# Forty-nine low parts of weight tiles move from GpSimd to VectorE in a float32 transformer kernel

## The chip, the cores and the metric

One Trainium2 chip, one of its cores. The metric is the device time of one execution of the whole program in microseconds (us), as a median of runs. Five engines take part: TensorE (PE in the profile, with PEld for its weight loads), VectorE (DVE), ScalarE (ACT), GpSimd (POOL) and SyncE (SP), which issues the weight loads.

## What is computed

The reference runs two transformer blocks in float32 on one sequence of 256 tokens of width 1024.

- First block, layer 0: a gated causal convolution of 31 taps over 768 channels beside an attention to 256 memory tokens, an output projection, and an MLP with squared ReLU of width 4096.
- First block, layer 1: shared keys and values (with a small compression MLP), sparse attention (compressed, selected and windowed branches, gated) beside a second memory attention, an output projection, and a second MLP of the same kind.
- Second block: "stick-breaking" attention beside a latent attention with rotary positions, an output projection, a gated MLP with a short causal convolution (`up` and `down`), and a gated embedding projection (`ple`, `ple_gate`).

```
x = first_block(x, mem, ...)      # two layers: x + mix @ w_out;  x + square(relu(norm(x) @ w_in)) @ w_out
return second_block(x, p_2, ...)  # x + norm(mix @ w_o);  x + norm(f @ w_down);  x + norm(g * e)
```

## The kernel before, in words

All activations lie in the on-chip memory (SBUF) in transposed form: 8 tiles of 128 channels by 256 tokens. Only the weights stream. They come in blocks (mostly 1024 rows by 256 columns, 1 MB) through a ring of four buffers, `ring`. SyncE issues the load of block b when block b-4 has been used up (`block_done`, L556).

**Weight tiles and their two parts.** A block holds two weight tiles w and w+1, each 128x1024. Products keep nearly float32 precision by splitting each operand into a high part, rounded to the matmul's format `fp32r`, and a low part, the difference. ScalarE makes the high part of tile w (`split_high`, L582, activation at L592). Then VectorE or GpSimd makes the low part, `ring - split_hi`, a tensor_tensor with both inputs in SBUF (`split_low`, L594, instruction at L600). TensorE multiplies high by high, high by low and low by high (`product`, L712, or `half_products`, L725; the matmuls stand at L707). High and low parts lie in four slots each (`SPLIT` = 4), so tile w+4 can be split when TensorE is done with tile w.

**Who makes a low part.** `low_part_engines()` (L396) writes down an engine for each of the 280 weight tiles. GpSimd has three shares: all tiles beside the convolution at the start (22 tiles, w = 4 to 25), the odd tiles beside the stick attention (6 tiles, in `s_in`, `s_lat`, `s_val`), and, of all other stages but `up`, each tile with w % 4 == 1 from w = 29 on (49 tiles). VectorE has the remaining 203.

**Where in an engine's program it happens.** GpSimd's program is little else: it walks through its tiles in order (`low_parts`, L1930), and each waits for its high part alone. VectorE's and ScalarE's programs are written out by hand in stage order, and a call `pump(stage, t)` (L1996 for VectorE, L1415 for ScalarE) stands behind the work on output tile t: it splits the tile four places later. On VectorE a pump of a tile that GpSimd has is empty. So the order of VectorE's work around a moved tile is fixed by these calls:

- `residual(stage, ...)` (L2033), used for `out0`, `out1` and the last eight tiles of each MLP: per tile t it adds the two halves of the result to x, then makes the low part of x's tile t-1 for the next stage (`low_of_x`, L2004), folds its squares into a sum (`fold`, L2015), then pumps t-1. `low_of_x` and `fold` read two SBUF operands.
- `mlp(l, ...)` (L2281): per tile of `mlp_in` it adds the two halves, applies ReLU and the norm's factor, makes the low part of hidden tile t-2 (`low_hidden`), and pumps t. In layer 1 a piece of `rope_angles` (L2252) follows in tiles 8 to 15.
- The start of layer 1 (L2318 to L2455): after `kv` it pumps tiles of `b_in`, forms the compression windows by 16 small additions (L2338), inverts the norm `ks` (L2341), makes two low parts of the values, pumps `b_in` 0 and 1 (L2348), then scales the keys (L2352), which ScalarE copies next. After query tile 7 it pumps `b_in` 4 and 5 (L2442), then forms `vbd` (L2446), which ScalarE copies ahead of the softmax work.
- The end of `down` (L2824 to L2843): residual additions with a `fold` each, then `pump("down", 21)`, the inversion of `postffn`, two more pumps and the norm.

TensorE's waits for a low part are on a count of the engine that makes it (`low_ready`, L573): `low_vector` or `low_gpsimd`. SyncE waits on the same counts for both halves of a block before it loads over it.

Of the kernel before, what the change touches and what calls it, by code (L numbers as in the profile page):

```python
# [26 lines left out]
SPLIT = 4  # L27
# [368 lines left out]
def low_part_engines():  # L396

    out = []
    for w, (_, _, (stage, t)) in enumerate(WEIGHT_TILES):
        beside_conv = w >= SPLIT and (stage in ("a_in", "mem_kv0", "mem_kv1") or (stage == "out0" and t < SPLIT))  # L400
        beside_sticks = w % 2 == 1 and (stage in ("s_lat", "s_val") or (stage == "s_in" and t >= SPLIT))
        out.append("gpsimd" if beside_conv or beside_sticks or (w >= SPLIT and w % 4 == 1 and stage != "up") else "vector")
    return out


LOW_ENGINE = low_part_engines()
LOW_COUNT = [LOW_ENGINE[:w + 1].count(LOW_ENGINE[w]) for w in range(NTILES)]
OUT = {name: n for n, name in enumerate(output_groups())}
# [2599 lines left out]
```

How the kernel before makes its waits and increments, by code:

```python
        def block_done(eng, b):  # L556
            name, r, _, c, _ = WEIGHT_BLOCKS[b]
            if name in DIRECT_LAST:
                wait_tile(eng, *DIRECT_LAST[name])
            elif name in DIRECT:
                if name == "gates":
                    eng.wait_ge(sem("gates.low_weights"), 1)
                elif r:
                    wait_tile(eng, name, 0)
                else:
                    eng.wait_ge(sem("compress_used"), 1 if name == "cmp_k" else 2)
            else:
                for half in range(2):
                    low_ready(eng, WEIGHTS_OF[tile_of(name, r, c)[0], tile_of(name, r, c)[1] + half])
# [1 line left out]
        def low_ready(eng, w):  # L573
            eng.wait_ge(sem(f"low_{LOW_ENGINE[w]}"), LOW_COUNT[w])
# [6 lines left out]
        def split_high(act, w):  # L582
            if w >= NTILES:
                return
            b = WEIGHT_TILES[w][0]
            act.wait_ge(sem(f"weights_in{b % RING}"), 16 * (b // RING + 1))
            if w >= SPLIT:
                wait_tile(act, *psum_of(*WEIGHT_TILES[w - SPLIT][2]))
            src, n = raw_weights(w)
            nc.scalar.activation(split_hi[:, w % SPLIT, 0:n], src, ACT.Copy).then_inc(sem("high_parts"), 1)
# [1 line left out]
        def split_low(eng, engine, w):  # L594
            if w >= NTILES or LOW_ENGINE[w] != engine:
                return
            eng.wait_ge(sem("high_parts"), w + 1)
            src, n = raw_weights(w)
            (nc.vector if engine == "vector" else nc.gpsimd).tensor_tensor(
```

## Time and profile before

| | |
|---|---|
| median of 3 runs | 1140.75 us (1138.5 to 1141.86) |
| the profiled execution's own time | 1141.37 us |
| its span, first to last instruction | 1139.6 us |
| TensorE busy | 1034.2 us, 91% of the span |
| VectorE busy | 814.0 us, 71% |
| ScalarE busy | 613.1 us, 54% |
| GpSimd busy | 192.8 us, 17% |
| low parts on VectorE (L600) | 203, mean 1231 ns |
| low parts on GpSimd (L600) | 77, mean 2464 ns |
| chain that ended last, by engine | PE 69%, DVE 22%, ACT 5%, issue 3% |

How to read it: "busy" is the time in which an engine executes. The granted clock is the share of its full 2.4 GHz that TensorE was given in a stretch. The chain of waits follows the program back from its last instruction. "Gap" or "idle before" is time in which an engine did nothing ahead of an instruction, with the instruction that ended the wait behind the arrow. Back-to-back instructions overlap a little: the pitch from start to start is shorter than the duration shown.

### The profile page before, as it was taken

Reading aid. Unit: us, or ns where it says so; the run is one execution under the profiler, and the core shown is the slowest. Engines: PE = TensorE matmul, PEld = TensorE weight load, DVE = VectorE, ACT = ScalarE, POOL = GpSimd, SP = SyncE. Lnnn points to the kernel's source line nnn. Section 1 sums busy time; section 2 is a strip of 40 time slices with the busy share of each in tenths; the row PEclk is TensorE's granted clock in tenths of the full one; section 3 lists DMA queues with packets and bytes.
Section 4 is the critical chain, followed back from the end, with each engine's and each line's share of the span. In section 5 each row is a group of like instructions: output and inputs, shape, how many; then the busy total and the mean of one; then the engine's idle time right before and its main releaser. Section 6 shows DMA issues by size and latency. Waiting matters only on the chain.

```text
span 1139.6 us, 17502 instructions
## 1 busy us (share of the span) xinstructions
PE 1034.2 (91%) x6654; PEld 931.8 (82%) x6654; DVE 814.0 (71%) x1571; ACT 613.1 (54%) x1147; POOL 192.8 (17%) x89
## 2 busy tenths in 40 slices
PE   5997689999999797878999999999988899999976
PEld 5996478888889796767887888898778799999865
DVE  4799778967768734685797766857645678777775
ACT  5552266654646545454655654665345566646555
POOL 1782002221212100000121222133000000010210
PEclk9996689999999897599999999999978999999978
DMA  8442024545445333101446555432301345554501
GB/s 350 155 176 76 1 74 181 196 180 204 167 181 185 112 116 112 37 1 37 157 179 219 181 189 185 184 119 77 137 13 74 130 177 180 184 192 169 194 33 37
DMA packets 22834, 158.28 MB, mean 139 GB/s; under 512 B 2528, under 2 KB 2784, under 8 KB 4448
## 3 DMA queue, kind: packets, MB, share of 16 engines
q1 hardware_dynamic: 21888, 153.51, 36.9%
q10 hardware_dynamic: 864, 3.66, 0.8%
q8 instruction: 53, 0.87, 0.3%
q14 instruction: 29, 0.24, 0.1%
HBM read 156.12 MB, written 1.05 MB: 138 GB/s over the span
## 4 chain that ended last, share of the span: by engine, by line
PE 69%; DVE 22%; ACT 5%; issue 3%; DMA 1%; DVEq 0%; ACTq 0%
PE bank L707 66%; DVE obank L1980 5%; DVE split_lo L600 3%; PE obank L707 2%; DVE square_sum L1972 1%; DVE temps L1972 1%; PE bank L840 1%; ACT split_hi L592 1%; DVE probs L1976 1%; DVE x L1972 1%; ACT L1388 1%; DVE tmp L1980 1%; DVE mlp_parts L1980 1%; DVE hidden_parts L1972 1%; DVE tmp L1972 1%
## 5 line engine op out<-in xcount | busy, mean ns | idle before, releaser
L707 PE MATMUL bank<-act_parts,split_hi 128*128 128x256 f32 (+1 forms) x1632 | 341.2, 305 | 32.5 <-DVE split_lo L600 13.1
L592 ACT ACTIVATE split_hi<-ring 128x1024 fp32r<-128x1024 f32 (+1 forms) x280 | 289.7, 1048 | 121.2 <-PE bank L707 120.7
L600 POOL TENSOR_TENSOR split_lo<-ring,split_hi 128x1024 fp32r<-128x1024 f32 (+1 forms) x77 | 189.3, 2464 | 910.7 <-ACT split_hi L592 910.7
L707 PEld LDWEIGHTS bank<-act_parts,split_hi 128*128 128x128 f32 x1632 | 270.3, 200 | 44.6 <-issue 28.7
L600 DVE TENSOR_TENSOR split_lo<-ring,split_hi 128x1024 fp32r<-128x1024 f32 (+1 forms) x203 | 247.8, 1231 | 38.0 <-ACT split_hi L592 37.1
L707 PE MATMUL bank<-hidden_parts,split_hi 128*128 128x512 f32 (+1 forms) x816 | 265.2, 377 | 2.9 <-DVE split_lo L600 2.2
L707 PE MATMUL bank<-act_parts,split_lo 128*128 128x256 f32 x880 | 256.1, 291 | 0.0
L707 PE MATMUL bank<-hidden_parts,split_lo 128*128 128x256 f32 x752 | 211.2, 281 | 0.0
L707 PE MATMUL bank<-mlp_parts,split_hi 128*128 128x512 f32 x512 | 181.0, 398 | 2.4 <-DVE mlp_parts L1980 2.4
L707 PEld LDWEIGHTS bank<-hidden_parts,split_hi 128*128 128x128 f32 x816 | 148.9, 188 | 34.0 <-DVE split_lo L600 2.8
L707 PEld LDWEIGHTS bank<-act_parts,split_lo 128*128 128x128 f32 x880 | 176.3, 200 | 0.0
L707 PE MATMUL bank<-mlp_parts,split_lo 128*128 128x256 f32 x512 | 143.2, 280 | 0.0
L707 PEld LDWEIGHTS bank<-hidden_parts,split_lo 128*128 128x128 f32 x752 | 141.0, 188 | 0.0
L707 PEld LDWEIGHTS bank<-mlp_parts,split_hi 128*128 128x128 f32 x512 | 96.1, 188 | 26.5 <-DVE mlp_parts L1980 3.3
L1972 DVE TENSOR_TENSOR x<-x,bank 128x256 f32<-128x256 f32 x160 | 67.0, 419 | 44.2 <-PE bank L707 40.7
L707 PEld LDWEIGHTS bank<-mlp_parts,split_lo 128*128 128x128 f32 x512 | 96.5, 189 | 0.0
L1980 DVE SCALAR_TENSOR_TENSOR obank<-temps,consts,obank 128x256 f32<-128x256 f32 x168 | 67.9, 482 | 0.0
L1980 DVE SCALAR_TENSOR_TENSOR tmp<-bank,consts,tmp 128x255 f32<-128x255 f32 (+1 forms) x88 | 39.9, 477 | 32.8 <-ACT tmp L1388 32.6
L1972 DVE TENSOR_TENSOR tmp<-bank,tmp 128x256 f32<-128x256 f32 x64 | 27.0, 422 | 38.8 <-ACT tmp L1391 36.4
L1388 ACT ACTIVATE tmp<-bank,consts 128x256 f32<-128x256 f32 x45 | 25.2, 561 | 54.1 <-PE bank L707 53.8
L840 PE MATMUL bank<-consts,probs 128*128 128x128 f32 x128 | 26.8, 346 | 27.4 <-DVE probs L1976 17.3
L840 PEld LDWEIGHTS bank<-consts,probs 128*128 128x128 f32 x128 | 18.0, 175 | 33.2 <-DVE probs L1976 19.4
(265 smaller groups left out, 1330.0 us busy)
## 6 DMA issues: line engine op xcount, KB each, us to landing
ring<-in_weights SPq DMA_DIRECT2D x141, 1024.0 KB, 4.8
ring<-in_weights SPq DMA_DIRECT2D x5, 768.0 KB, 4.1
x<-in_x ACTq DMA_DIRECT2D x1, 1024.0 KB, 7.7
y<-in_mem ACTq DMA_DIRECT2D x1, 1024.0 KB, 9.8
out<-x SPq DMA_DIRECT2D x4, 256.0 KB, 2.6
consts<-in_consts ACTq DMA_DIRECT2D x1, 885.0 KB, 13.1
ring<-in_weights SPq DMA_DIRECT2D x1, 512.0 KB, 3.6
consts<-in_consts ACTq DMA_DIRECT2D x1, 260.0 KB, 7.8
```

The source lines that it names most:

```text
L592: nc.scalar.activation(split_hi[:, w % SPLIT, 0:n], src, ACT.Copy).then_inc(sem("high_parts"), 1)
L600: (nc.vector if engine == "vector" else nc.gpsimd).tensor_tensor(split_lo[:, w % SPLIT, 0:n], src, split_hi[:, w % SPLIT, 0:n].bitcast(F32 ...
L707: return nc.tensor.matmul(dst, lhsT, rhs, start=start, stop=stop)
L840: return nc.tensor.transpose(dst, src, const("ident")[0:k, 0:k])
L1388: return nc.scalar.activation(dst, src, func, bias=bias, scale=scale, **more)
L1972: return nc.vector.tensor_tensor(dst, a, b, op)
L1976: return nc.vector.tensor_scalar(dst, a, s, None, op)
L1980: return nc.vector.scalar_tensor_tensor(out=dst, in0=a, scalar=s, in1=b, op0=op0, op1=op1)
```

## The change

The engine table loses its third clause. The 49 tiles named above go to VectorE's pumps, GpSimd keeps 28, and VectorE has 252. No other line changes; the pumps, their order and the semaphores' meaning stay, with the counts on both semaphores following the table.

```diff
--- before.py
+++ after.py
@@ -399,7 +399,7 @@
     for w, (_, _, (stage, t)) in enumerate(WEIGHT_TILES):
         beside_conv = w >= SPLIT and (stage in ("a_in", "mem_kv0", "mem_kv1") or (stage == "out0" and t < SPLIT))
         beside_sticks = w % 2 == 1 and (stage in ("s_lat", "s_val") or (stage == "s_in" and t >= SPLIT))
-        out.append("gpsimd" if beside_conv or beside_sticks or (w >= SPLIT and w % 4 == 1 and stage != "up") else "vector")
+        out.append("gpsimd" if beside_conv or beside_sticks else "vector")
     return out
```

The moved tiles by stage: `out0` 1, `mlp_in0` 8, `mlp_out0` 8, `kv` 1, `b_in` 2, `out1` 2, `mlp_in1` 8, `mlp_out1` 8, `s_in` 1, `o` 2, `down` 6, `ple_gate` 2. Forty-seven are 128x1024; two, in `down`, are 128x768.

## Rows read from the trace of the kernel before

**Rows 1.** The page: a costliest-groups line and a DMA-issue line.
```profile
L600 POOL TENSOR_TENSOR split_lo<-ring,split_hi 128x1024 fp32r<-128x1024 f32 (+1 forms) x77 | 189.3, 2464 | 910.7 <-ACT split_hi L592 910.7
...
ring<-in_weights SPq DMA_DIRECT2D x141, 1024.0 KB, 4.8
```

**Rows 2.** Busy time by stretch: length, PE, PEld, DVE, ACT, POOL, clock, DMA share, GB/s.
```profile
175.00:345.00 170.00, 170.00 (x968) 147.98 (x967) 129.27 (x206) 96.52 (x166) 35.77 (x16) 1.00 0.50 185
...
430.00:522.00 92.00, 72.16 (x420) 64.75 (x420) 58.14 (x177) 46.44 (x138) 2.34 (x1) 0.76 0.11 41
...
550.00:612.00 62.00, 58.87 (x334) 50.83 (x335) 52.21 (x88) 36.62 (x72) 12.06 (x5) 1.00 0.49 175
```

**Rows 3.** Timeline, end of `out0`, VectorE and GpSimd: start, duration, engine, line, operation.
```profile
161.82 0.87 DVE L1972 TENSOR_TENSOR x<-x,bank 128x256 f32<-128x256 f32 x2
...
161.92 2.41 POOL L600 TENSOR_TENSOR split_lo<-ring,split_hi 128x1024 fp32r<-128x1024 f32 x1 [64.85 <-ACT split_hi L592]
...
162.61 2.00 DVE L1980 SCALAR_TENSOR_TENSOR mlp_parts<-x,consts,mlp_parts 128x256 fp32r<-128x256 f32 x1
...
164.86 0.86 DVE L1972 TENSOR_TENSOR x<-x,bank 128x256 f32<-128x256 f32 x2
...
167.51 0.87 DVE L1972 TENSOR_TENSOR x<-x,bank 128x256 f32<-128x256 f32 x2
```

**Rows 4.** Timeline, start of layer 1, windows and keys.
```profile
378.39 4.69 DVE L1972 TENSOR_TENSOR temps<-temps,consts 64x128 f32<-64x128 f32 x8
...
379.97 2.46 DVE L1972 TENSOR_TENSOR temps<-temps,consts 64x128 f32<-64x128 f32 x1
...
383.37 1.97 PE L707 MATMUL bank<-consts,rc 128*64 128x128 f32 x16 [5.24 <-DVE rc L1989]
...
384.46 1.22 DVE L600 TENSOR_TENSOR split_lo<-ring,split_hi 128x1024 fp32r<-128x1024 f32 x1
385.60 0.87 DVE L1980 SCALAR_TENSOR_TENSOR temps<-temps,consts,bank 128x256 f32<-128x256 f32 x2
...
390.19 0.38 ACT L1388 ACTIVATE sq<-bank 128x256 f32<-128x256 f32 x1 [1.11 <-PE bank L707]
...
391.56 1.06 ACT L592 ACTIVATE split_hi<-ring 128x1024 fp32r<-128x1024 f32 x1
```

**Rows 5.** Timeline, ahead of the sparse attention.
```profile
443.31 1.23 DVE L600 TENSOR_TENSOR split_lo<-ring,split_hi 128x1024 fp32r<-128x1024 f32 x1
444.57 1.02 DVE L1972 TENSOR_TENSOR temps<-bank,consts 96x384 f32<-96x384 f32 x2
...
454.50 0.48 PE L840 MATMUL bank<-consts,probs 128*128 128x128 f32 x1 [8.09 <-DVE probs L1976]
```

**Rows 6.** Timeline, first half of the second MLP.
```profile
564.03 1.22 DVE L600 TENSOR_TENSOR split_lo<-ring,split_hi 128x1024 fp32r<-128x1024 f32 x1
...
566.30 1.22 DVE L600 TENSOR_TENSOR split_lo<-ring,split_hi 128x1024 fp32r<-128x1024 f32 x1
...
601.41 0.50 PE L707 MATMUL bank<-hidden_parts,split_hi 128*128 128x512 f32 x1 [0.98 <-DVE split_lo L600]
...
604.99 3.38 DVE L600 TENSOR_TENSOR split_lo<-ring,split_hi 128x1024 fp32r<-128x1024 f32 x1
...
608.43 0.51 PE L707 MATMUL bank<-hidden_parts,split_hi 128*128 128x512 f32 x1 [1.17 <-DVE split_lo L600]
```

**Rows 7.** Timeline, TensorE at the end of three residual stages.
```profile
173.35 0.50 PE L707 MATMUL bank<-mlp_parts,split_hi 128*128 128x512 f32 x1 [1.25 <-DVE mlp_parts L1980]
...
550.98 0.49 PE L707 MATMUL bank<-mlp_parts,split_hi 128*128 128x512 f32 x1 [1.14 <-DVE mlp_parts L1980]
...
735.09 0.38 PE L707 MATMUL bank<-act_parts,split_hi 128*128 128x256 f32 x1 [1.21 <-DVE act_parts L1980]
```

**Rows 8.** Timeline, end of `down`.
```profile
1085.67 2.06 DVE L1972 TENSOR_TENSOR square_sum<-square_sum,sq 128x256 f32<-128x256 f32 x1
...
1089.49 0.27 PE L707 MATMUL bank<-consts,square_sum 128*128 128x1 f32 x1 [0.38 <-DVE square_sum L1972]
```

## The prediction

> **What bounds the kernel now.** I read the page first. TensorE is busy for nine tenths of the span and carries most of the chain that ended last; VectorE carries a fifth of it. So VectorE matters only where TensorE waits for it, and the question is where those places are. The busy times by stretch answer that [rows 2]. In the first MLP TensorE is busy for 170.00 us of 170.00. No saving or added work on VectorE can show there unless VectorE falls behind. The same picture holds in the later part of the second MLP and in `up` and `down`. The stretch from 550 to 612 us is another: TensorE 58.87 of 62 us, VectorE 52.21, so VectorE nearly keeps it from running. The stretch from 430 to 522 is short chains between engines, with a mean granted clock of 0.76.
>
> The timeline then shows what GpSimd's low parts do to VectorE [rows 3]. GpSimd starts one at 161.92 and ends at 164.33. VectorE reaches an operation on two SBUF operands at 162.61 and ends it only at 164.61, a quarter of a microsecond after GpSimd. Of the 49 tiles that move, 25 have such a stretched VectorE instruction beside them, from this one (2.00 us) to the last (2.06 us [rows 8]). Where VectorE's work in that moment reads a PSUM bank or nothing, nothing is stretched. So the work handed to GpSimd takes up to about 2.2 us out of VectorE, and the same tile on VectorE itself costs a pitch of 1.14 us (from 384.46 to 385.60, back to back [rows 4]).
>
> The Trainium skill, page "SBUF — State Buffer", section "SBUF: two separate sides", states an exclusive lock: a GpSimd instruction and a VectorE one with two SBUF inputs hold a shared port pair for the whole instruction. The trace agrees in kind. By that rule the stretched parts vanish with GpSimd's instruction and the sum below stands; without it the stretched records would mean something else, and the slower rival below would hold.
>
> **The change part by part.** It removes 49 GpSimd instructions (mean 2.46 us [rows 1]) and adds 49 to VectorE at 1.14 us of pitch, some 56 us of work, less the stretches that vanish. It adds no instruction, no DMA and no semaphore.
>
> *Most tiles: nothing.* In the stretches where TensorE runs without a gap, 968 matmuls in 170 us [rows 2] at 16 a tile make 2.8 us a tile. VectorE's cycle in `mlp_in` with a low part in each tile is 2.27 us (564.03 to 566.30 [rows 6]), and a tile is pumped several tiles ahead of its use. VectorE thus keeps up with every low part of its own. If that cover went, each moved tile would cost 1.14 us.
>
> *End of `out0`, of `out1` and of `mlp_out1`: gain 1.2 us.* With GpSimd's tile beside it a cycle of `residual` takes 3.04 us (161.82 to 164.86); with the low part on VectorE it takes 2.65 (164.86 to 167.51 [rows 3]). That is 0.39 us. VectorE is behind TensorE there, and TensorE's waits at the end of these stages are 1.25, 1.14 and 1.21 us [rows 7], so each of the three gets about 0.4. Bounds: nothing, and 3.6 us, the whole of the waits. I take the cycle difference, since it is measured at the spot. The end of `mlp_out0` also has a stall, but TensorE sets VectorE's pace there, and I count nothing.
>
> *Windows and keys in layer 1: gain 2.0 us.* Eight small additions take 4.69 us, one of them 2.46 (GpSimd works beside it); the other seven share 2.2, so about 2.1 us are stall [rows 4]. Behind them stands the inversion that ends TensorE's wait of 5.24 us at 383.37. That wait shrinks by 2.1. The stalling tile, w = 105, is pumped only after the inversion, ahead of the scaling of the keys. There VectorE is 2.1 us earlier and spends 1.14 more, so the keys' scaling starts near 384.6, where it was 385.60. ScalarE copies the keys, then waited 1.11 us for TensorE at 390.19 [rows 4]. TensorE now comes 2.1 us earlier and the copies end 1.0 us earlier, which uses up that 1.11 almost exactly. I take 2.0. Bounds: 1.0 (if the keys' copies set the pace alone) and 2.4.
>
> SyncE's queue must be looked at here, for it loads a block when both halves have been used. It now waits for w = 105 rather than 104, from 385.68 to about 384.7, and a load lands 4.8 us after its issue [rows 1], at 389.5. ScalarE wants that block at 391.56 now [rows 4] and at 389.5 after. It just fits; a few tenths might be lost, and the bound of 1.0 holds them. The other loads are issued long before their use.
>
> *Ahead of the sparse attention: loss 1.1 us.* Tile w = 109 was made by GpSimd with nobody disturbed. Now it stands between w = 108 (443.31) and the forming of `vbd` (444.57) [rows 5], and from `vbd` a chain of ScalarE and VectorE steps runs without slack to TensorE's wait of 8.09 us at 454.50. The pitch is 1.14, all of it on the path. Bounds 0 and 1.23.
>
> *Second MLP, 550 to 612: gain 2.1 us.* VectorE is behind from the start (it waits for the norm) and carries the rotary angles as well. Up to 608 it is stalled four times by moved tiles. The last is a low part of 3.38 us against 1.22 [rows 6]. Each is a stall of about 2.1 us, and three of the four tiles take 1.14 on VectorE by then. VectorE is thus ahead by some 5 us at 608. TensorE's two waits for low parts, 0.98 and 1.17 us [rows 6], should both go: 2.15. Bounds 0 and 2.15, as TensorE has no other wait there.
>
> *End of `down`: gain 0.4 us.* A fold is held for 1.65 us of its 2.06 at 1085.67; TensorE waits 0.38 us for the last fold at 1089.49 [rows 8], and cannot gain more, since its filler matmuls end there. The tile w = 273 is now made between that fold and the inversion, in time that VectorE spends waiting for TensorE and ScalarE. If it were late it would cost at most 1.14.
>
> *Moved tiles in `kv`, `s_in`, `o`, `ple_gate` and `down`'s middle: nothing.* VectorE waits for another engine behind each of them; a low part that lost this cover would cost 1.14.
>
> Sum: 1.2 + 2.0 - 1.1 + 2.1 + 0.4 = 4.6 us gained. The profiled execution took 1141.4 us, so 1136.8 after; the median of the runs lies 0.6 lower, which makes 1136.2.
>
> **The rivals.**
>
> *A. The gain is partly given back by TensorE's clock in layer 1's attention.* From 430 to 522 us the mean clock is 0.76, and 72.16 us of TensorE's work lie there [rows 2]. Its wait of 8.09 us gets longer and all work is shifted in time. At a mean clock of 0.73 the same work takes 72.16 x 0.76 / 0.73 = 75.1 us, 3.0 more. That gives 1139.2. For it: the level is already broken there. Against it: the added 1.1 us is small beside 8.09, and the shift can just as well turn out in favour (then near 1133.5).
>
> *B. The stalls on the path are not worth their length*, because TensorE's waits have another cause right behind. The gains then fall to their lower halves: 0.6 + 1.0 - 1.1 + 1.0 + 0.2 = 1.7 us, time 1139.1. For it: the waits at the ends of the residual stages are only partly VectorE's fault. Against it: the timeline has VectorE back to back ahead of each.
>
> *C. Slower: the stretch is not caused by GpSimd and stays.* Then VectorE gets 1.14 us more for each moved tile and nothing back. It decides where VectorE already holds TensorE: four tiles in 550 to 612 us (4.6), one at each of three residual ends (3.4), one ahead of the sparse attention (1.1). Together 9.1 us, time 1149.9. The point from which this decides is a stall saved of less than 1.14 us a tile. For it speaks only VectorE's load, 52.21 of 62 us [rows 2]. Against it: the ends of the stretched instructions follow GpSimd's ends [rows 3]. The Trainium skill, page "Perfetto Trace Analysis", section "Optimizing Scalar/DVE Operations", says that with a saturated VectorE it may make sense to offload work to GpSimd, and adds that the shared port may undo the help. By its first half this change would be wrong in that stretch; the rows bear out the second.
>
> *D. It does nothing*, because all moved tiles are covered: 1140.8. The two waits for low parts and the 5.24 us wait speak against it.
>
> **How the numbers follow.** The forecast has 0.66, A in its bad form 0.12, B 0.14, C 0.04, D 0.04. A measurement of this kernel can tell about 0.3%, 3.4 us, from no change: below 1137.3 counts as faster. The forecast's own spread crosses that line in about a tenth of its cases, and A's good form lies within it. So faster 0.66, same 0.30, slower 0.04. The bounds of all terms together would reach from 8.4 us gained to 0.1 gained; all at one end at once is unlikely. The range reaches over A and B, and on the other side to the good form of the clock: 1133.0 to 1139.6.
>
> **What would show it right or wrong.** Right: GpSimd at 28 low parts, VectorE at 252 with a mean near 1.2 us and no two-operand instruction above 1.3 us outside convolution and sticks; TensorE's wait before the `ks` broadcast near 3.1 us; no wait for low parts around 600 us; the wait ahead of the sparse attention near 9.2; the waits that end the three residual stages near 0.8. Wrong: TensorE waits for low parts in the MLPs or in `down`; stretched instructions that remain; a granted clock in 430 to 522 us clearly off 0.76; or a wait of ScalarE for the weight load near 389 us.

## The result, and the profile after

The changed kernel is slower. Its median is 1148.51 us against 1139.62 for the kernel before in the same comparison, ratio 1.0082 with a 95% interval of 1.0054 to 1.0110; a second comparison (e11 below) gave 1147.45 against 1136.5, ratio 1.0088 [1.0060, 1.0116]. The forecast had been 1136.2, faster, with a range that ended at 1139.6. Ratios here and below are taken over a kernel's fast executions alone (here without the two of 1167.85 and 1331.04 us), so they need not be the quotient of the medians.

The profiled execution took 1144.93 us, its span is 1143.1 us, and its mean granted clock is 0.926; before it was 0.933. The page's two lines on the low parts, first VectorE's, then GpSimd's [rows 1]:

```profile
L600 DVE TENSOR_TENSOR split_lo<-ring,split_hi 128x1024 fp32r<-128x1024 f32 (+1 forms) x252 | 303.2, 1213 | 44.1 <-ACT split_hi L592 43.3
...
L600 POOL TENSOR_TENSOR split_lo<-ring,split_hi 128x1024 fp32r<-128x1024 f32 x28 | 68.9, 2478 | 463.9 <-ACT split_hi L592 463.9
```

252 and 28, as the table of engines says, and VectorE's mean fell from 1231 to 1213 ns: the part that had been stretched to 3.38 us is gone.

Now the waits that the forecast named, from the timeline of the changed kernel. First TensorE:

```profile
170.29 0.50 PE L707 MATMUL bank<-mlp_parts,split_hi 128*128 128x512 f32 x1 [0.80 <-DVE mlp_parts L1980]
...
378.19 0.33 PE L707 MATMUL bank<-consts,rc 128*64 128x128 f32 x2 [3.13 <-DVE rc L1989]
...
460.17 0.48 PE L840 MATMUL bank<-consts,probs 128*128 128x128 f32 x1 [9.23 <-DVE probs L1976]
...
557.61 0.50 PE L707 MATMUL bank<-mlp_parts,split_hi 128*128 128x512 f32 x1 [0.76 <-DVE mlp_parts L1980]
...
740.29 0.38 PE L707 MATMUL bank<-act_parts,split_hi 128*128 128x256 f32 x1 [0.73 <-DVE act_parts L1980]
```

Each did what the forecast said: the three residual ends 1.25, 1.14 and 1.21 to 0.80, 0.76 and 0.73 [rows 7]; the wait ahead of the `ks` broadcast 5.24 to 3.13 [rows 4]; the one ahead of the sparse attention 8.09 to 9.23 [rows 5]. The two waits for low parts near 600 us [rows 6] and the one of 0.38 at the end of `down` [rows 8] are not in the trace any more. VectorE shows why, in the same timeline:

```profile
372.63 5.28 DVE L1972 TENSOR_TENSOR temps<-temps,consts 64x128 f32<-64x128 f32 x16
...
447.85 2.36 DVE L600 TENSOR_TENSOR split_lo<-ring,split_hi 128x1024 fp32r<-128x1024 f32 x2
450.24 1.02 DVE L1972 TENSOR_TENSOR temps<-bank,consts 96x384 f32<-96x384 f32 x2
...
599.98 1.22 DVE L600 TENSOR_TENSOR split_lo<-ring,split_hi 128x1024 fp32r<-128x1024 f32 x1
...
602.24 1.22 DVE L600 TENSOR_TENSOR split_lo<-ring,split_hi 128x1024 fp32r<-128x1024 f32 x1
...
1092.01 0.99 DVE L1972 TENSOR_TENSOR square_sum<-square_sum,sq 128x256 f32<-128x256 f32 x2
```

All sixteen window additions take 5.28 us, where they had taken 7.39, the last eight of them 4.69; two low parts in a row stand ahead of the forming of `vbd`; low parts in the second MLP follow each other in 2.26 us; the fold at the end of `down` takes half a microsecond where it took 2.06.

So every wait moved as forecast, and still the program is longer. One more TensorE wait tells where to look. It stands 9.5 us behind the `ks` broadcast, ahead of the first `b_in` tile that shares its loop with the key compression (`linear_beside_compress`), and ends when VectorE has written `query_stack`. First the kernel before, then the changed one, TensorE's timeline:

```profile
392.83 0.60 PE L707 MATMUL bank<-temps,ring 128*128 128x32 f32 x4 [0.82 <-DVE query_stack L1980]
393.27 0.48 PE L707 MATMUL bank<-act_parts,split_hi 128*128 128x256 f32 x2
...
393.71 0.53 PE L707 MATMUL bank<-temps,ring 128*128 128x32 f32 x4
...
394.51 0.53 PE L707 MATMUL bank<-temps,ring 128*128 128x32 f32 x4
```

```profile
387.71 0.60 PE L707 MATMUL bank<-temps,ring 128*128 128x32 f32 x4 [2.03 <-DVE query_stack L1980]
388.15 0.49 PE L707 MATMUL bank<-act_parts,split_hi 128*128 128x256 f32 x2
...
388.59 0.53 PE L707 MATMUL bank<-temps,ring 128*128 128x32 f32 x4
...
389.44 0.90 PE L707 MATMUL bank<-temps,ring 128*128 128x32 f32 x4
```

The same four matmuls take 0.53 us, and from 389.44 on 0.90: TensorE has fallen to the lower of its two levels, 1.2 GHz. Busy time by stretch shows how long. The first row of each kernel runs from the `ks` broadcast to this wait's end, the second is the start of the work behind it, the third all of it up to the first transposes of the sparse attention (columns as in [rows 2]; first before, then changed):

```profile
383.37:392.83 9.46, 8.64 (x57) 7.89 (x57) 4.24 (x8) 5.08 (x10) 0.00 (x0) 0.69 0.33 111
392.83:416.30 23.47, 23.47 (x198) 22.74 (x198) 11.79 (x26) 10.90 (x29) 0.00 (x0) 1.00 0.18 56
392.83:454.50 61.67, 53.58 (x409) 50.81 (x409) 26.21 (x68) 28.83 (x75) 2.34 (x1) 0.89 0.29 106
```

```profile
378.19:387.71 9.52, 7.49 (x57) 6.82 (x57) 5.22 (x9) 4.93 (x9) 0.00 (x0) 0.82 0.33 110
387.71:413.20 25.49, 25.49 (x125) 25.16 (x126) 9.82 (x20) 8.55 (x21) 0.00 (x0) 0.53 0.15 48
387.71:460.17 72.46, 63.23 (x408) 60.62 (x409) 27.48 (x69) 29.01 (x75) 0.00 (x0) 0.75 0.25 90
```

In both, TensorE is busy for every microsecond of the second row. Before it does 198 matmuls in 23.47 us at full clock; now 125 in 25.49 us with a clock of 0.53. The third row takes 72.46 us where it took 61.67. Of the 10.8 us, 1.14 are the longer wait for w = 109; the other 9.6 are the clock (TensorE's busy time in the row grew from 53.58 to 63.23), more than all that the change saves.

### The profile page after: what moved, and what is told of

It reads as the page before. It is cut to its first block, busy times and chain, and to the rows that moved or that the text cites. A ratio compares the mean times of both kernels' runs of the same rounds, so it can differ in the third digit from the quotient of the medians.

```text
span 1143.1 us, 17502 instructions
## 1 busy us (share of the span) xinstructions
PE 1042.2 (91%) x6654; PEld 940.7 (82%) x6654; DVE 828.0 (72%) x1620; ACT 614.4 (54%) x1147; POOL 72.5 (6%) x40
## 4 chain that ended last, share of the span: by engine, by line
PE 75%; DVE 17%; ACT 4%; issue 2%; DMA 1%; DVEq 0%; ACTq 0%
PE bank L707 72%; DVE obank L1980 5%; PE obank L707 2%; DVE split_lo L600 2%; PE bank L840 1%; ACT split_hi L592 1%; DVE probs L1976 1%; ACT L1388 1%; DVE temps L1972 1%; DMA consts<-in_consts 1%; DVE square_sum L1972 1%; DVE rowmax L2506 1%; DVE x L1972 1%; ACT sq L1388 1%; ACT act_parts L1391 0%
## 5 line engine op out<-in xcount | busy, mean ns | idle before, releaser
L600 DVE TENSOR_TENSOR split_lo<-ring,split_hi 128x1024 fp32r<-128x1024 f32 (+1 forms) x252 | 303.2, 1213 | 44.1 <-ACT split_hi L592 43.3
L600 POOL TENSOR_TENSOR split_lo<-ring,split_hi 128x1024 fp32r<-128x1024 f32 x28 | 68.9, 2478 | 463.9 <-ACT split_hi L592 463.9
```

What stands on the lines that cost most here:

```text
L600: (nc.vector if engine == "vector" else nc.gpsimd).tensor_tensor(split_lo[:, w % SPLIT, 0:n], src, split_hi[:, w % SPLIT, 0:n].bitcast(F32 ...
```

## The experiments

Each ran beside the kernel before on one chip. Two figures recur. "Wait 1" is TensorE's wait ahead of the `ks` broadcast, "wait 2" the one ahead of the first tile beside the compression, and "stretch" the time from the end of wait 2 to the first transposes of the sparse attention, all from the timelines. "What the clock took" is one minus the mean granted clock, times the span, as the median of a kernel's runs. It counts half clock inside a wait too, where it costs nothing, so only kernels with the same idle matmuls can be compared by it.

| kernel | median us (before) | ratio [95%] | wait 1, 2 | stretch, its clock | clock took |
|---|---|---|---|---|---|
| before, profiled first | | | 5.24, 0.82 | 61.67, 0.89 | 76.4 (this run) |
| changed, profiled first | 1148.51 (1139.62) | 1.0082 [1.0054, 1.0110] | 3.13, 2.03 | 72.46, 0.75 | 85.9 |
| e1 w = 101, 105 kept | 1136.74 (1136.13) | 0.9990 [0.9964, 1.0015] | 5.25, 0.82 | 59.74, 0.92 | 72.6 |
| e2 only 101, 105 moved | 1149.67 (1136.13) | 1.0138 [1.0090, 1.0185] | 3.15, 2.00 | 71.28, 0.75 | 87.2 |
| e3 changed, 2.2 us later | 1149.54 (1136.13) | 1.0103 [1.0074, 1.0132] | 3.14, 1.99 | 72.41, 0.75 | 84.9 |
| e4 wait 2 filled in part | 1146.75 (1136.13) | 1.0084 [1.0057, 1.0111] | 0.55, 1.88 | 72.43, 0.75 | 83.5 |
| e5 changed, both filled | 1133.45 (1137.70) | 0.9965 [0.9949, 0.9981] | none | 61.28, 0.90 | 67.9 |
| e6 w = 105, 109 kept | 1135.81 (1137.70) | 0.9994 [0.9978, 1.0010] | 5.24, 0.82 | 61.68, 0.88 | 74.8 |
| e7 three filled, 109 kept | 1129.25 (1137.70) | 0.9938 [0.9917, 0.9959] | none | 60.18, 0.94 | 59.8 |
| e8 before, both filled | 1140.00 (1137.70) | 1.0028 [1.0005, 1.0050] | 0.49, none | 58.50, 0.93 | 69.4 |
| e9 before again | 1133.72 (1136.50) | 0.9973 [0.9933, 1.0012] | 5.24, 0.81 | 58.56, 0.93 | 67.9 |
| e10 before, wait 1 filled | 1151.34 (1136.50) | 1.0111 [1.0052, 1.0170] | 0.48, 2.36 | 72.83, 0.74 | 81.6 |
| e11 changed again | 1147.45 (1136.50) | 1.0088 [1.0060, 1.0116] | 3.13, 2.02 | 73.66, 0.74 | 86.1 |
| e12 e7, one more filled | 1130.95 (1136.50) | 0.9932 [0.9901, 0.9963] | none | 60.11, 0.94 | 58.7 |

The kernel before, on these chips, has medians of what the clock took of 71.4, 70.4 and 71.4 us.

### e1: two tiles stay with GpSimd

```diff
-        out.append("gpsimd" if beside_conv or beside_sticks else "vector")
+        out.append("gpsimd" if beside_conv or beside_sticks or w in (101, 105) else "vector")
```

> The changed kernel, but the two b_in tiles w = 101 and 105 stay with GpSimd. Theory 1 (TensorE's clock: in the changed kernel it is at half level from 389.3 to 413.2 us, right behind a wait of 2.03 us at 387.71 that was 0.82 before, and this costs about 8.5 us net): without the two tiles the start of layer 1 runs as in the kernel before, the long half-clock stretch is gone, and the time is some 2.6 us below the kernel before (the forecast gain less the 2.0 for windows and keys), ratio 0.998. Theory 2 (VectorE's 49 more low parts cost the time wherever it is short): two tiles of 49 change little, ratio 1.008 as measured. Theory 3 (the clock, but decided by the instant at which the waits of TensorE fall, not by the wait's length): the waits still come 3 us earlier than in the kernel before, and the ratio can be either; the stretch of half clock in 378 to 455 us is then still unlike that of the kernel before.

Measured: 0.9990, the waits and the clock of the kernel before. Forty-seven of the 49 tiles moved, and no time lost. Theory 2 falls.

### e2: only these two move

```diff
-        out.append("gpsimd" if beside_conv or beside_sticks or (w >= SPLIT and w % 4 == 1 and stage != "up") else "vector")
+        out.append("gpsimd" if beside_conv or beside_sticks or (w >= SPLIT and w % 4 == 1 and stage != "up" and w not in (101, 105)) else "vector")
```

> The kernel before, with only the two b_in tiles w = 101 and 105 moved to VectorE. Theory 1: the wait ahead of the ks broadcast falls from 5.24 to about 3.1 us, the wait behind it rises to about 2 us, and the long half-clock stretch appears: ratio about 1.005 (8.5 lost less 2.0 gained, 1146 us). Theory 2: no change beyond 0.1%, ratio 0.999 to 1.000. Theory 3: either; the two waits are as in theory 1, but the clock behind them depends on where they fall.

Measured: 1.0138, all of the loss. Waits 3.15 and 2.00, and the busy time of the stretch has the clock of the changed kernel:

```profile
391.18:462.46 71.28, 63.18 (x409) 60.42 (x409) 26.26 (x68) 28.89 (x75) 2.35 (x1) 0.75 0.25 91
```

Two tiles out of 49 carry the loss. The interval of 1.0090 to 1.0185 overlaps with that of the whole change, so what the other 47 bring back can't be read from this pair. The loss is larger than the 1.005 expected. That had been made with a price of 8.5 us for the stretch, taken against the first trace of the kernel before, where it takes 61.67 us. In a second trace of the same kernel (e9) it takes 58.56, and e2's is 12.7 us longer than that. Over whole runs the clock took 87.2 us, 15.8 more than in the kernel before.

### e3: everything later by 2 us

```diff
+            DELAYED = range(8, 18)
...
+                        if stage == "mlp_in0" and t in DELAYED and k == 0:
+                            mm(dst[:, :], w[0][:, k, :], parts[:, :, k, :])
                         last = half_products(dst, w, k, parts, k == 0, k == kts - 1)
```

> The changed kernel, with ten matmuls of 512 columns repeated in mlp_in0 (tiles 8 to 17, the first matmul of each tile done twice), where TensorE works without a gap: all that follows comes about 2.4 us later, and nothing else is changed. Theories 1 and 2: 2.4 us are added, ratio 1.010. Theory 3: the wait of about 2 us at the start of layer 1 is the same in length and only comes 2.4 us later, and the half-clock stretch of 23.9 us behind it shrinks or goes: about 1142 us, ratio 1.002 to 1.003.

Measured: 1.0103. The first MLP takes 184.9 us where it took 182.7, all else of the changed kernel is there again, and the half clock is as long. The moment at which the wait falls was not what decided, at least not over these 2.2 us. The other traces say the same: wait 2 ends between 387.7 and 391.2 us in the six kernels that have the long half clock, and between 389.3 and 392.8 us in the eight that don't.

### e4 and e5: idle matmuls in the two waits

```diff
             linear("b_in", 0, 2, projected)
+            keep_busy(take("ks.bc", 0), 12)
             head_bcast("ks")
...
             scores("mem1", UNITS["mem1"][1], 1)
+            own_obank(UNITS["mem1"][0].group)
+            keep_busy(obank(UNITS["mem1"][0].group), 7)
             linear_beside_compress(3, "k", 0)
```

e5 has 14 and 15 in place of 12 and 7.

> The changed kernel, with idle matmuls in TensorE's two waits at the start of layer 1: 12 ahead of the ks broadcast (its wait is 3.13 us), 7 ahead of the first b_in tile beside the compression (2.03 us). Theories 1 and 3: no half clock between 378 and 425 us, so about 13 us of half-clock time less and 1139 to 1142 us, ratio at or below 1.002. Theory 2: TensorE's waits are only filled, ratio 1.008.

> The changed kernel with 14 idle matmuls ahead of the ks broadcast and 15 ahead of the first b_in tile beside the compression. With 12 and 7 the first wait was down to 0.55 us and half clock behind it was gone, but 1.88 us of the second wait were left and the clock fell behind it as before, to 413.1. Theory 1 (the second wait sets off the long half-clock stretch, and the compression's own matmuls then keep it up): with no wait left there, no half clock between 378 and 425 us, some 12 us of TensorE's time back in 389 to 413, and a time of 1137 to 1141 us, ratio 0.998 to 1.003. Rival (the work of that stretch, not the wait, brings the clock down once it comes early enough): half clock from about 389 to 413 us as before, ratio 1.008.

e4 missed its aim, and that made it useful. With the first wait filled the clock stayed full through it, so TensorE did the 57 matmuls behind it in less time and came to wait 2 earlier. VectorE and ScalarE ended that wait when they do in the changed kernel (9.52 us after the broadcast in both), and seven idle matmuls left 1.88 us of it. TensorE's timeline of e4:

```profile
384.09 1.68 PE L707 MATMUL obank<-cbias_b,ident_b 128*128 128x512 bf16 x7
387.66 0.60 PE L707 MATMUL bank<-temps,ring 128*128 128x32 f32 x4 [1.88 <-DVE query_stack L1983]
...
389.42 0.90 PE L707 MATMUL bank<-temps,ring 128*128 128x32 f32 x4
```

The half clock came as in the changed kernel. In e5 fifteen idle matmuls reach to the end:

```profile
386.65 3.41 PE L707 MATMUL obank<-cbias_b,ident_b 128*128 128x512 bf16 x15
390.20 0.60 PE L707 MATMUL bank<-temps,ring 128*128 128x32 f32 x4
...
391.08 0.53 PE L707 MATMUL bank<-temps,ring 128*128 128x32 f32 x4
...
391.88 0.53 PE L707 MATMUL bank<-temps,ring 128*128 128x32 f32 x4
```

No matmul of the stretch starts earlier for it, but they keep 0.53 us; the stretch takes 61.28 us instead of 72.43, and the kernel is faster than the one before, 0.9965. The rival, that the work itself brings on the long half clock once it comes this early, falls: the same work at the same place starts at the full level and keeps it for some 39 us.

What e5 does not show is that the clock falls only behind a wait. It also falls later in this stretch, for 3 to 10 us at a time, while TensorE is busy throughout. The first row is the kernel before, where this comes at about 416.5 us; the second is the changed kernel, where it comes at about 437.5 (columns as in [rows 2]). e5 has such a piece too, from about 429.5 to 436 us. Why these come where they do is open.

```profile
400.00:425.00 25.00, 25.00 (x192) 23.20 (x191) 10.02 (x23) 11.64 (x29) 0.00 (x0) 0.93 0.37 132
```

```profile
425.00:450.00 25.00, 25.00 (x189) 24.04 (x187) 8.10 (x23) 10.14 (x22) 0.00 (x0) 0.86 0.32 128
```

### e10: no tile moved, only wait 1 filled

```diff
             linear("b_in", 0, 2, projected)
+            keep_busy(take("ks.bc", 0), 22)
             head_bcast("ks")
```

> The kernel before, no tile moved, with 22 idle matmuls in the wait of 5.24 us ahead of the ks broadcast and none in the second. Theory 1 (a second wait of 2 us sets the long half-clock stretch off, whatever makes it): the clock is full through the first wait, TensorE comes earlier to the first b_in tile beside the compression and waits 3 to 3.5 us there, and the half clock of some 24 us appears though no tile was moved: ratio 1.006 to 1.012. Rival (the moved tiles do it in some other way): ratio 1.000 to 1.003 and no half clock in 390 to 415 us, as in e8_before_filled.

Measured: 1.0111. This is the kernel before with all its tiles where they were, and it has the loss. TensorE's timeline:

```profile
382.10 0.33 PE L707 MATMUL bank<-consts,rc 128*64 128x128 f32 x2 [0.48 <-DVE rc L1990]
...
390.48 0.67 PE L707 MATMUL bank<-temps,ring 128*128 128x32 f32 x4 [2.36 <-DVE query_stack L1981]
...
391.75 0.90 PE L707 MATMUL bank<-temps,ring 128*128 128x32 f32 x4
```

The wait was 2.36 us and not the 3 to 3.5 expected, since VectorE ended it 8.38 us after the broadcast; it was enough. With e5, where the same work starts 0.28 us earlier in the execution and has no wait ahead of it, this closes the case: a wait 2 of about 2 us sets the long half clock off, whoever makes it, and without that wait the long one doesn't come, tiles moved or not.

### e8: the kernel before with both filled

The edit is that of e5, with 22 and 15.

> The kernel before, with 22 idle matmuls ahead of the ks broadcast (wait 5.24 us) and 15 ahead of the first b_in tile beside the compression. The half clock in 382.4 to 389.3 us goes, and the chain of VectorE and ScalarE sets the pace as it did: 0 to 2 us faster, ratio 0.998 to 1.000. Against e5_filled_wholly it shows what the moved tiles are worth when the clock is the same in both: e5_filled_wholly should be 4 to 5 us faster than this.

Measured: 1.0028, outside what was expected of it. Its profiled execution took 1136.1 us and its stretch 58.50 us at clock 0.93, but its median is 1140.0. The clock took 64.7 us in the profiled execution and 69.4 in the median of all; where it took more, I have no trace of. A part of the miss is in the trace: its second MLP takes 185.65 us, 1.5 more than in the kernel before, for a reason that stays open (see below). Against e5 on the same chip it is 6.6 us slower, where 4 to 5 were expected. Time less what the clock took is, as the median over runs, 1070.5 for e8 and 1065.9 for e5: 4.6 us, of which those 1.5 can't be put down to the moved tiles.

### e6, e9 and e11: what else the clock takes

e6 is e1 with `w in (105, 109)`; e9 and e11 are unchanged kernels.

> The changed kernel, but w = 105 (the tile that stalls the window additions) and w = 109 (which GpSimd made with nobody disturbed, ahead of the sparse attention) stay with GpSimd; w = 101 goes to VectorE. If w = 105 alone is the cause: waits of 5.2 and 0.8 us at the start of layer 1 as in the kernel before, no long half-clock stretch, the wait ahead of the sparse attention 8.1 us, and the other parts of the forecast gain are left: 1.2 + 2.1 + 0.4 = 3.7 us, ratio 0.997. If w = 101 takes part: the first wait is nearer 3 us and the ratio 1.005 or more.

> The kernel before, unchanged, for a second trace of it. In its runs so far the clock took 66 to 85 us (one minus the mean clock, times the span), mostly 67 to 72, and 76.4 in the profiled execution the forecast was made on. Expected if that execution was only an unlucky one: the waits as before (5.24, 0.82, 8.09, 0.98, 1.17 us) and fewer or shorter half-clock stretches; time 1133 to 1141 us, ratio 1.000.

> The changed kernel, unchanged, on the same chip as the others of this set: ratio 1.008 to 1.012, the clock takes 83 to 88 us, and half clock of 23.9 us behind the wait of 2.0 us. If the ratio is below 1.004 the slowdown belongs to a chip or an hour and not to the kernel.

e6 has the waits that were expected, 5.24, 0.82 and 8.09, so w = 105 alone is the tile behind wait 1, and w = 109 the one behind the sparse wait. But its ratio is 0.9994 where 0.997 was expected. Time less what the clock took is 1061.5 us against 1066.7 for the kernel before on that chip, 5.2 less; the clock took 74.8 instead of 70.4. Most of what was saved went to the clock again. In its trace this is in short stretches at many places, such as 414 to 418 and 431 to 438 us, both with TensorE busy throughout.

e9 shows the size of that lottery. It is the same kernel as before, and a second trace of it has the same waits to 0.1 us in the places named, and another clock: the stretch takes 58.56 us instead of 61.67, and the next one, up to the first matmul of `out1`, 68.64 us instead of 70.02 (e9's rows):

```profile
390.71:449.27 58.56, 50.47 (x408) 48.02 (x409) 26.19 (x68) 28.83 (x75) 2.36 (x1) 0.93 0.31 111
449.27:517.91 68.64, 55.13 (x311) 48.34 (x311) 48.51 (x147) 35.35 (x108) 0.00 (x0) 0.78 0.05 16
```

In e11's runs the clock took 83.4 to 87.2 us, in those of the kernel before beside it 67 to 85 with a median of 71.4. So the loss is no accident of a chip. By this measure the change takes 1066.0 - 1061.8 = 4.2 us of work away and gives 86.1 - 71.4 = 14.7 us to the clock. The two traces put it in one place: the stretch takes 73.66 us in e11 and 58.56 in e9.

### e7 and e12: more waits filled

e7 is e5 with w = 109 kept by GpSimd and 38 idle matmuls ahead of the first transposes of the sparse attention; e12 has 19 more ahead of those of layer 0's memory attention.

```diff
-                pe.wait_ge(sem("nsa.scaled"), n + 1)
                 dst = take("nsa", "T", n)
+                if n == 0:
+                    keep_busy(dst, 38)
+                pe.wait_ge(sem("nsa.scaled"), n + 1)
```

```diff
+                if kind == "mem0" and n == 0:
+                    pe.wait_ge(sem("bf16_consts"), 1)
+                    keep_busy(take(kind, "T", n), 19)
                 wait_emptied(pe, kind, "S", n)
-                dst = take(kind, "T", n)
+                dst = bank(kind, "T", n) if kind == "mem0" and n == 0 else take(kind, "T", n)
```

> As e5_filled_wholly, with w = 109 kept by GpSimd and 38 idle matmuls in TensorE's wait ahead of the sparse attention (8.1 us). If the clock goes by the waits there too: half clock in 450 to 485 us, 30.7 us long in the changed kernel, is mostly gone; TensorE's matmuls there count for half as long, but the chain of ScalarE and VectorE sets part of the pace, so some 3 to 8 us less than e5_filled_wholly, ratio 0.992 to 0.996. If not: as e5_filled_wholly less 1.1 us.

> As e7_filled_and_109, and 19 idle matmuls in TensorE's wait of 4.7 us ahead of the first transposes of layer 0's memory attention, behind which 30.7 us of half clock lie in every trace. If the clock goes by the waits there too: a good part of that stretch goes, 2 to 5 us less than e7_filled_and_109, ratio 0.989 to 0.992. If the work behind the wait (small matmuls with waits of 1 to 2 us between them) brings the clock down in any case: as e7_filled_and_109, 0.994.

e7 beats both kernels, 0.9938 [0.9917, 0.9959]. Busy time of its two stretches:

```profile
389.25:449.43 60.18, 60.18 (x447) 53.28 (x447) 26.38 (x68) 29.10 (x76) 2.34 (x1) 0.94 0.30 108
449.43:515.38 65.95, 51.03 (x311) 44.51 (x311) 48.46 (x147) 35.41 (x108) 0.00 (x0) 0.84 0.05 17
```

e7 is 4.2 us faster than e5, within the 3 to 8 expected. In the traces the stretch is 1.1 us shorter (w = 109), and behind the filled wait the 311 matmuls of the sparse attention come in 65.95 us instead of e5's 68.63. They have waits of 1 to 2 us for ScalarE and VectorE between them in which the clock still falls. e12 shows that limit: its waits behind the filled one in layer 0 became longer by what the matmuls became shorter, the pieces of that stage before and behind its filled wait take 22.17 and 24.43 us as in the kernel before, and the ratio 0.9932 cannot be told from e7's. A filled wait pays most where TensorE is the bound behind it, as beside the compression (11 us of stretch in e5), less where other engines share it (2.7 us in e7), and in layer 0 nothing.

## Why the prediction was wrong

**Right but for one term: the work.** The forecast of the work was good. In the profiled pair the `out0` wait shrank by 0.45 us; windows and keys gained 2.11 (27.33 to 25.22 us from the last `hidden_parts` wait to the broadcast) less 0.06 behind it, where 2.0 was said; the wait ahead of the sparse attention grew by 1.14, where 1.1 was said; the end of `out1` gained 0.38; from there to the end of the second MLP it is 1.43 us; `down`'s wait of 0.38 is gone. These add up to about 3.6 us. By the runs it is 4.2 us (e11) or 4.6 (e5 against e8, with the 1.5 named there). The sum said 4.6, so it comes close partly by luck: the MLP's term of 2.1, with 0.4 for its end, was too large. (A slip without weight: the bounds of the terms add up to 0.2 and 8.6 us gained, not 0.1 and 8.4.) The busy time of that stage, before and after:

```profile
550.98:735.09 184.11, 180.75 (x1040) 157.60 (x1040) 140.94 (x237) 107.09 (x183) 38.77 (x16) 1.00 0.51 183
```

```profile
557.61:740.29 182.68, 181.95 (x1040) 158.50 (x1040) 147.76 (x253) 107.45 (x183) 0.00 (x0) 1.00 0.52 185
```

Both waits are gone, yet TensorE is busy 1.2 us longer for the same 1040 matmuls: in the 60 us from the second wait on, the 512-column ones had followed each other in 231 ns on the mean, and at the same place now in 235. It is no accident of one trace. The kernels whose MLP tiles lie with GpSimd (before, e2, e9, e10) have 231 ns and 183.95 to 184.11 us for the stage; those with the tiles on VectorE have about 235 to 237 ns and 182.68 to 182.75 us. But e8 has 236 to 237 ns with GpSimd's tiles and both waits there, and its stage took 185.65 us, so the tiles alone do not decide it. Why, I did not find.

**Right: the rival C was rightly small.** No stretched instruction stayed outside the convolution and the sticks, and no load came late enough to matter: ScalarE waited 0.18 us for the block that the forecast had called just in time. The trace of the changed kernel, ScalarE:

```profile
386.60 1.06 ACT L592 ACTIVATE split_hi<-ring 128x1024 fp32r<-128x1024 f32 x1 [0.18 <-DMA ring<-in_weights]
```

It was slower all the same, by a road that had no rival on the slower side.

**Wrong: the step "windows and keys in layer 1: gain 2.0 us".** The size was right, and the bounds of 1.0 and 2.4 were of waits alone. The step took for granted that 2 us less of waiting are 2 us less of time, and the forecast did not ask what TensorE does with its clock where the wait had been. Before, the wait of 5.24 us ended at half clock: 57 matmuls took up 8.64 of the 9.46 us behind it, and left a wait of 0.82. With 3.13 us the clock is back sooner (0.82 in those 9.52 us, not 0.69), the 57 matmuls are done in 7.49 us, but ScalarE and VectorE release the next ones no earlier. What TensorE gained it spent in wait 2, and behind that wait began 25 us in which TensorE is the only bound. The row of 0.82 us at 392.83 was in the trace and not in the forecast.

**Wrong: rival A's place and price.** It said that the clock would give part of the gain back; the clock took more than the gain. But it was placed in the sparse attention, from 430 to 522 us, because the level was "already broken there", and priced at 3.0 us with a chance of 0.12. The mean clock from 430 to 522 us is 0.76 again. The price came from the stretch ahead of it, where TensorE has no waits and the clock had been whole for its first 23 us: 9.6 us in the profiled pair, 15.1 with the longer sparse wait between e9 and e11. A stretch that already has a low clock has little to lose; one at full clock in which TensorE is the bound can lose nearly half its speed (198 matmuls in 23.47 us against 125 in 25.49).

**Wrong: the base.** The forecast was taken off an execution of 1141.4 us in which the clock took 76.4 us, and off a median of three runs close to it. In the four comparisons since, the medians of the kernel before are 1136.1 to 1139.6 us, with 70.4 to 71.4 us taken by the clock in the three for which I have it. That put the forecast 1 to 5 us too high, and made the miss look smaller than it was.

**The port.** The part of the forecast that leaned on the Trainium skill, page "SBUF — State Buffer", section "SBUF: two separate sides", holds: with GpSimd's instruction gone, every two-operand VectorE instruction named has its short duration, 5.28 us for all sixteen additions. The skill's page "TensorE: Matmul & The Clock Gate", section "Part 1: The HAM clock gate (the "warmup" mystery)", says that sustained matmuls bring the array back to its full clock. Here the trace does not agree: 25.49 us with TensorE busy throughout ran at 0.53.

## What to carry to other kernels

Before a wait of TensorE is shortened, follow TensorE to its next wait and read the granted clock of what lies behind that: where TensorE is the only bound there and at full clock, a wait that grows from 0.8 to 2 us can cost more than the whole gain. Idle matmuls in such a wait are cheap (0.22 us each here), but they must leave no more than a short rest of it (0.49 and 0.55 us left of wait 1 did no harm in e8 and e4, 1.88 us left of wait 2 did), and must be counted again whenever the work ahead of them speeds up. And take the base of a forecast from several executions and their clocks, not from the one with the trace.

## What the runs showed of the hardware

- One piece of work, two clocks. The matmuls beside the compression (four of 32 columns, then three of 256, again and again, with no wait) stayed at the full level for 23 us when they began there (before, e1, e5 to e9, e12), and at the half level for some 24 to 27 us when they fell there in their first microseconds (changed, e2, e3, e4, e10, e11). TensorE was busy throughout in both.
- What tipped it in these traces was a wait of 1.88 to 2.36 us; waits of 0.81 and 0.82 us at the same place did not. Where between them it turns, no run shows.
- The clock also fell without any wait, for 3 to 10 us, later in the same stretch: mean clock 0.93 and 0.86 in rows in which TensorE was busy for 25.00 of 25.00 us. So a wait is one way to the half level and not the only one.
- The clock takes a different amount in each execution of the same kernel: 67 to 76 us in 30 runs of the kernel before on one chip, that is most of its spread from 1133 to 1142 us.
